# Seven tile products for eight in part of an fp32 down projection, with a new head and tail

## The reference

```
h = h + relu(RMSNorm(h) @ W_up)^2 @ W_down      # W_up 2048 x 8192, W_down 8192 x 2048
out = RMSNorm(h)
```

## Time and profile before

| | |
|---|---|
| three executions | 2035.08, 2036.14, 2038.41 us; median 2036.14 |
| the profiled execution | 2037.86 us |
| its span | 2036.1 us |
| granted TensorE clock, mean | 0.998 |
| instructions | 26601 |
| weight loads of the down projection | 128 of 512 KB, median 4.8 us from issue to landing |
| of the up projection | 128 of 512 KB, 3.9 us |

### The profile page before, as it was taken

The page is one execution under the profiler, slowest core; times in us unless marked ns, Lnnn a source line. Parts: engine busy times, 40 slices in busy tenths (PEclk is TensorE's granted clock), DMA queues, the critical chain, the costliest instruction groups (busy, mean ns, idle before and its releaser), DMA issues.

```text
span 2036.1 us, 26601 instructions
## 1 busy us (share of the span) xinstructions
PE 2018.9 (99%) x9378; PEld 1666.9 (82%) x9378; DVE 1384.1 (68%) x1735; ACT 1034.7 (51%) x1454; POOL 278.6 (14%) x417
## 2 busy tenths in 40 slices
PE   9999999999999999999999999999999999999997
PEld 7888888888888877888887888888888888888886
DVE  6665878687665678885688877666556556655664
ACT  5444546464544567663566644544344434433443
POOL 4000111111110233330033311011001000000000
PEclk9999999999999999999999999999999999999999
DMA  8757666666666666666666677766666666666663
GB/s 274 219 178 208 195 194 191 195 192 192 175 208 208 183 191 198 193 197 209 183 185 185 194 255 233 229 211 204 215 195 203 223 197 193 221 205 185 219 216 135
DMA packets 202726, 411.49 MB, mean 202 GB/s; under 512 B 15264, under 2 KB 15360, under 8 KB 201200
## 3 DMA queue, kind: packets, MB, share of 16 engines
q1 hardware_dynamic: 188656, 364.56, 58.0%
q0 software_dynamic: 13776, 44.96, 7.6%
q10 hardware_dynamic: 176, 0.40, 0.1%
HBM read 379.91 MB, written 2.16 MB: 188 GB/s over the span
## 4 chain that ended last, share of the span: by engine, by line
PE 91%; DVE 3%; ACT 2%; issue 2%; ACTq 1%; DVEq 0%; POOLq 0%; POOL 0%; DMA 0%
PE acc L307 28%; PE acc L309 28%; PE acc L308 28%; DVE lo L274 1%; PE x L999 1%; ACT hi L268 1%; ACT W L1313 1%; PE tr L948 1%; PE tr L342 1%; PE x L931 1%; DVE XCT L1697 0%; PE x L937 0%; PE x L867 0%; ACTq L1314 0%; PE tr L950 0%
## 5 line engine op out<-in xcount | busy, mean ns | idle before, releaser
L274 DVE TENSOR_TENSOR lo<-raw,hi 128x1024 fp32r<-128x1024 f32 x688 | 837.8, 1233 | 457.9 <-ACT hi L268 450.0
L268 ACT ACTIVATE hi<-raw 128x1024 fp32r<-128x1024 f32 x688 | 718.8, 1057 | 623.3 <-PE acc L309 561.4
L307 PE MATMUL acc<-hi,LAh 128*128 128x512 f32 x1840 | 727.9, 396 | 0.0
L309 PE MATMUL acc<-hi,LAl 128*128 128x512 f32 x1840 | 717.3, 390 | 0.0
L308 PE MATMUL acc<-lo,LAh 128*128 128x512 f32 x1840 | 716.6, 389 | 0.0
L307 PEld LDWEIGHTS acc<-hi,LAh 128*128 128x128 f32 x1840 | 345.5, 188 | 75.3 <-issue 3.2
L309 PEld LDWEIGHTS acc<-hi,LAl 128*128 128x128 f32 x1840 | 345.3, 188 | 73.1
L308 PEld LDWEIGHTS acc<-lo,LAh 128*128 128x128 f32 x1840 | 345.6, 188 | 70.6 <-issue 1.1
L307 PE MATMUL acc<-hi,LBh 128*128 128x512 f32 x896 | 349.8, 390 | 0.0
L309 PE MATMUL acc<-hi,LBl 128*128 128x512 f32 x896 | 348.7, 389 | 0.0
L308 PE MATMUL acc<-lo,LBh 128*128 128x512 f32 x896 | 348.6, 389 | 0.0
(11 more groups left out here) (343 smaller groups left out, 1324.4 us busy)
## 6 DMA issues: line engine op xcount, KB each, us to landing
raw<-w_in SPq DMA_DIRECT2D x304, 512.0 KB, 4.3
raw<-w_up SPq DMA_DIRECT2D x128, 512.0 KB, 3.9
raw<-w_down SPq DMA_DIRECT2D x128, 512.0 KB, 4.8
raw<-w_proj_ssm SPq DMA_DIRECT2D x64, 512.0 KB, 4.7
raw<-w_proj_nsa SPq DMA_DIRECT2D x32, 512.0 KB, 4.7
raw<-w_out SPq DMA_DIRECT2D x32, 512.0 KB, 5.5
W<-acs_rows POOLq DMA_DIRECT2D x8, 1024.0 KB, 6.7
W<-TB POOLq DMA_DIRECT2D x48, 128.0 KB, 4.1
```

The lines of the kernel that those rows point to most:

```text
L268: act.activation(hi[:, sl, :, :], raw[:, sl, :, :], ACT.Copy).then_inc(s_hi, 1)
L274: dve.tensor_tensor(lo[:, sl, :, :], raw[:, sl, :, :], hi[:, sl, :, :].bitcast(F32), ALU.subtract).then_inc(s_lo, 1)
L307: pe.matmul(o, xh, wh, start=(k == 0), stop=False)
L309: x = pe.matmul(o, xl, wh, start=False, stop=(k == KT - 1))
```

## The change

A chunk pair and a depth pair of blocks (tiles j = 0 and 1, that is blocks 0 to 3) together with the two row halves form a 2 x 2 by 2 x 2 product of tiles. The change makes it with seven products for eight (Winograd's form of Strassen's scheme), for two of the eight depth pairs of seven of the eight chunk pairs: both pairs of phases 0 to 2 and the first of phase 3.

- A pair of chunks ("quad") is now 20 ring positions: four ordinary tiles of the first chunk (n, j = 2 to 5), a group a, b, p, q, two ordinary tiles (j = 6, 7), a second group, and six ordinary tiles of the second chunk. a and b are the loaded tiles of the same depth in both chunks; VectorE makes p and q from them in their ring slots with four half-tile additions. p and q aren't loaded. Of b only the second half is split.
- The seven products go to acc and to the four banks B1, B6, B7, B5. Sums of the activation's row tiles are made and split once a phase (slots 13 to 15). In slots 13 to 17 of a quad VectorE adds the product banks into H (first_sums to fourth_sums).
- The load of a tile into the slot of an a waits for one low part more, that of b.
- ScalarE's and VectorE's loops over phases 1 and 2 are written out. XDT and ZT are no longer kept in the MLP; the row sums' parts lie there.
- Head: POOL makes the identity first, TensorE warms from then on (9, 8 and 12 transposes), the first tile is split in two halves, x(1) and x(2) are turned after the first and second tile, and SP's order of loads is changed to match.
- Tail: POOL's power is replaced by a square root on ScalarE (with one such root ahead of the last phase) and a reciprocal and one Newton step on VectorE (root_inverse); the second half's output is scaled and stored in four pieces.

```diff
+UP, QUAD, TWO = 32, 20, 16
+PHASE = UP + 2 * QUAD
+G_MLP = 8 * C_MLP
+G_END = G_MLP + 3 * PHASE + UP + QUAD + TWO
+QUAD_ORDER = ([("n", 0, j) for j in (2, 3, 4, 5)] + [(c, 0, 0) for c in "abpq"] + [("n", 0, j) for j in (6, 7)] +
+              [(c, 0, 1) for c in "abpq"] + [("n", 1, j) for j in (2, 3, 4, 5, 6, 7)])
+TWO_ORDER = [("n", c, j) for c in range(2) for j in range(8)]
+def tile_of(i, x):
+    if x < UP:
+        return "n", x // 8, x % 8, x // 4 + 1
+    q, y = divmod(x - UP, QUAD)
+    order = TWO_ORDER if (q == 1 and i is LAST) else QUAD_ORDER
+    kind, c, j = order[y]
+    loads = UP // 4 + 4 * q + sum(order[z][0] not in "pq" for z in range(y % 4, y + 1, 4))
+    return kind, 4 + 2 * q + (c if kind == "n" else 0), j, loads
+LAST = 3
...
+        SF = TH
+        U3, U5, U2, U4 = (GA[:, 1, NC * n:NC * (n + 1)] for n in range(4))
+        U35 = GA[:, 1, 0:2 * NC].rearrange("p (n c) -> p n c", n=2)
+        B1, B6, B7, B5 = TR[0], TR[1], X6, X7
...
             load_group(sp, C_KC, 0, w_in, 0, KC0)
+            load_group(sp, C_KC, 1, w_in, 0, KC0)
             load_x(1)
-            load_group(sp, C_KC, 1, w_in, 0, KC0)
             load_group(sp, C_KC, 2, w_in, 0, KC0)
             load_x(2)
             load_group(sp, C_KC, 3, w_in, 0, KC0)
-            load_group(sp, C_KC, 4, w_in, 0, KC0)
             load_x(3)
-            for j in (5, 6, 7):
+            for j in (4, 5, 6, 7):
...
+            def load_tile(sp, i, x):
+                kind, c, j, _ = tile_of(i, x)
+                if kind in "pq":
+                    return
+                before = tile_of(i, x - RING)[0] if x >= RING else "n"
+                sp.wait_ge(s_lo, G_MLP + PHASE * i + x - RING + (2 if before == "a" else 1))
+                if c < 4:
+                    src = w_up[:, 2 * j:2 * j + 2, ds(D * i + NC * c, NC)]
+                else:
+                    c0 = NC * (c - 4 + (kind == "b"))
+                    src = w_dn[:, ds(KT * i + 2 * j, 2), c0:c0 + NC]
+                sp.dma_start(raw[:, x % RING, :, :], src).then_inc(s_raw[x % RING], 16)
+            def load_phase(sp, i):
+                for x in range(PHASE if i is not LAST else PHASE - 4):
+                    load_tile(sp, i, x)
+            with sp.Fori(0, 3) as i:
+                load_phase(sp, i)
+            load_phase(sp, LAST)
...
+            pool.affine_select(identf[:, :], identf[:, :], [[-1, P]], ALU.not_equal, 1.0, base=0, channel_multiplier=1)
+            pool.drain().then_inc(s_idn, 1)
...
-            for t in range(2):
-                pool.wait_ge(s_v, t + 2)
-                pool.tensor_tensor(RS[:, t:t + 1], VV[:, t:t + 1], mhalf[:, 0:1], ALU.pow).then_inc(s_fr, 1)
...
+            pe.wait_ge(s_idn, 1)
+            warm(9)
...
-            warm(9)
+            warm(8)
             turn_x(0)
-            warm(5)
-            turn_x(1)
-            mm_chunk(pe, C_KC, 0, LAh, LAl, {0: [lambda: turn_x(2)], 3: [lambda: turn_x(3)]},
-                     need={0: [(s_x0, 1)], 1: [(s_trd, 1)], 2: [(s_trd, 2)], 4: [(s_trd, 3)], 6: [(s_trd, 4)]})
+            warm(12)
+            pe.wait_ge(s_x0, 1)
+            pe.wait_ge(s_g0l, 1)
+            mm_chunk(pe, C_KC, 0, LAh, LAl, {0: [lambda: turn_x(1)], 1: [lambda: turn_x(2)], 3: [lambda: turn_x(3)]},
+                     need={1: [(s_trd, 1)], 2: [(s_trd, 2)], 4: [(s_trd, 3)], 6: [(s_trd, 4)]})
...
+            def product(o, xh, xl, g, kk, start, stop):
+                sl = g % RING
+                pe.matmul(o[:, :], xh, hi[:, sl, kk, :], start=start, stop=False)
+                pe.matmul(o[:, :], xh, lo[:, sl, kk, :], start=False, stop=False)
+                return pe.matmul(o[:, :], xl, hi[:, sl, kk, :], start=False, stop=stop)
+            def seven_products(g, u, p0, p1):
+                def rows(t, k):
+                    return LAh[:, 2 * u + k, t * P:(t + 1) * P], LAl[:, 2 * u + k, t * P:(t + 1) * P]
+                def sums(n):
+                    return LSh[:, n - 1, u * P:(u + 1) * P], LSl[:, n - 1, u * P:(u + 1) * P]
+                one, two = u == 0, u == 1
+                pe.wait_ge(s_lo, g + 1)
+                product(B1, *rows(0, 0), g, 0, one, two)
+                product(acc[p0][0], *rows(0, 1), g, 1, False, two).then_inc(s_mm, 1)
+                pe.wait_ge(s_lo, g + 2)
+                product(acc[p1][0], *sums(4), g + 1, 1, one, False).then_inc(s_mm, 1)
+                pe.wait_ge(s_lo, g + 3)
+                product(B5, *sums(1), g + 2, 0, one, two)
+                product(B7, *sums(3), g + 2, 1, one, two).then_inc(s_mm, 1)
+                pe.wait_ge(s_lo, g + 4)
+                product(B6, *sums(2), g + 3, 0, one, two)
+                product(acc[p0][1], *rows(1, 1), g + 3, 1, False, two).then_inc(s_mm, 1)
+            def four_blocks(i, q):
+                g, C = G_MLP + PHASE * i + UP + QUAD * q, C_MLP + 8 * i + 4 + 2 * q
+                p0, p1 = C % 2, (C + 1) % 2
+                pe.wait_ge(s_acc, C - 1)
+                for y, (kind, c, j) in enumerate(QUAD_ORDER):
+                    if kind == "a":
+                        if j == 0:
+                            pe.wait_ge(s_acc, C)
+                            pe.wait_ge(s_sfl, i + 1)
+                            if 2 * i + q:
+                                pe.wait_ge(s_ux, 2 * i + q)
+                        seven_products(g + y, j, p0, p1)
+                    elif kind == "n":
+                        if c == 0 and j == 6:
+                            pe.wait_ge(s_trd, E_MLP + 4 * i + 4)
+                        mlp_group(g + y, (p0, p1)[c], j, LAh, LAl, t_first=((j == 2 and c == 0), j == 2), last=((c, j) == (1, 7)))
...
+            act.wait_ge(s_raw[0], 16)
+            act.activation(hi[:, 0, 0, :], raw[:, 0, 0, :], ACT.Copy).then_inc(s_g0h, 1)
...
+                kind, _, u, loads = tile_of(i, x)
+                g, sl = G_MLP + PHASE * i + x, x % RING
+                if kind in "pq":
+                    act.wait_ge(s_wt, 8 * i + 4 * ((x - UP) // QUAD) + 2 * u + (1 if kind == "p" else 2))
+                else:
+                    act.wait_ge(s_raw[sl], 16 * (2 * C_MLP + 16 * i + loads))
+                act.wait_ge(s_mm, g - RING + 1)
+                k0 = 1 if kind == "b" else 0
+                act.activation(hi[:, sl, k0:2, :], raw[:, sl, k0:2, :], ACT.Copy).then_inc(s_hi, 1)
...
+            def split_tile(i, x):
+                kind, _, u, loads = tile_of(i, x)
+                g, sl = G_MLP + PHASE * i + x, x % RING
+                sa, sb_, sp_, sq = ((x - "abpq".find(kind) + n) % RING for n in range(4))
+                if kind == "a":
+                    dve.wait_ge(s_lo, g - 1)
+                    for n in (sa, sb_):
+                        dve.wait_ge(s_raw[n], 16 * (2 * C_MLP + 16 * i + tile_of(i, x + (n == sb_))[3]))
+                    for kk, (m, mk) in enumerate(((sa, 0), (sb_, 0))):
+                        y = dve.tensor_tensor(raw[:, sp_, kk, :], raw[:, sb_, kk, :], raw[:, m, mk, :], ALU.subtract)
+                    y.then_inc(s_wt, 1)
+                if kind == "b":
+                    dve.wait_ge(s_lo, g - 1)
+                    dve.wait_ge(s_wt, 8 * i + 4 * ((x - UP) // QUAD) + 2 * u + 1)
+                    dve.tensor_tensor(raw[:, sq, 0, :], raw[:, sp_, 1, :], raw[:, sa, 0, :], ALU.add)
+                    dve.drain()
+                    dve.tensor_tensor(raw[:, sq, 1, :], raw[:, sa, 1, :], raw[:, sq, 0, :], ALU.subtract).then_inc(s_wt, 1)
+                dve.wait_ge(s_hi, g + 1)
+                k0 = 1 if kind == "b" else 0
+                dve.tensor_tensor(lo[:, sl, k0:2, :], raw[:, sl, k0:2, :], hi[:, sl, k0:2, :].bitcast(F32),
+                                  ALU.subtract).then_inc(s_lo, 1)
+            def row_sums(i):
+                r = [TSS[0].rearrange("p (a q r j) -> p r q a j", q=2, r=4, j=32)[:, n, :, :, :] for n in range(4)]
...
+                dve.drain()
...
+            def row_sums_low(i):
+                dve.wait_ge(s_sfh, i + 1)
+                dve.tensor_tensor(LSl[:, :, :], SF, LSh[:, :, :].bitcast(F32), ALU.subtract).then_inc(s_sfl, 1)
+            def add_blocks(g, C, n):
+                dve.wait_ge(s_mm, g)
+                dve.drain()
+                for t in range(2):
+                    x = dve.tensor_tensor(H[:, t, NC * n:NC * (n + 1)], acc[C % 2][t][:, :], H[:, t, NC * n:NC * (n + 1)], ALU.add)
+                x.then_inc(s_acc, 1)
+            def first_sums(n):
...
+                dve.tensor_tensor(h, B1[:, :], h, ALU.add)
+                dve.tensor_copy(U2, B1[:, :])
+                dve.drain()
+                dve.tensor_tensor(U2, B6[:, :], U2, ALU.add)
+            def second_sums():
+                dve.drain()
+                dve.tensor_tensor(U3, B7[:, :], U2, ALU.add)
+                dve.tensor_tensor(U4, B5[:, :], U2, ALU.add)
+            def third_sums(n):
+                h = H[:, 0, NC * n + NC:NC * n + 2 * NC]
+                dve.drain()
```

(66 more changed lines are left out.)

159 lines of the change are left out of this document (105 added, 54 removed).

## The result

The changed kernel took **2062.43 us** (median of four executions, 2059.20 to 2065.27) against 2036.39 of the kernel before (four, 2035.08 to 2038.41): the ratio is 1.0127, with a 95% interval of 1.0115 to 1.0140. The forecast was 2065.0 and slower.

What follows compares the result with a forecast made beforehand. TensorE was taken to set the pace. Stalls of 38.4 us less 9.5 gained give +28.9, head and tail 0: 2066.8 from the profiled 2037.9, or 2065.0 at the median's level; range 2050 to 2087.

Steps and rivals of the forecast that it cites:

- The bound and the 42 matmuls: MLP: TensorE alone sets the pace; 42 matmuls removed at 0.227 us each gain 9.5 us if its feeders stay ahead.
- the marks that were named: Signs of being right: 42 fewer matmuls, MLP idle 38 us, pauses 2.5 to 3.5, w_down wait over 30, first-quad q 2.
- the pause before q in first quads: First quads: q waits behind the split of the last activation block on ScalarE and VectorE, 2.1 us.
- The long pause: Every quad: TensorE waits for the first ordinary tile behind the second group's q, 2.8 us.
- The chain: Reload behind the second group: issue, landing, high part, low part, TensorE's start, against at most 3.5 us of matmuls in store.
- The sum of a first quad: First quad of a phase: all its TensorE stalls together, 6.4 us.
- The small ones: Second group: b 0.65 (second quads 0.25), p 0.45 us; second quads' tile behind the first group 0.7 us.
- The sum: MLP: stalls of four first quads at 6.4 and three second quads at 4.2 us, 38.4 us lost.
- the quick end: MLP: every landing at 3.7 us with quicker drains, +20 us; as the case of cheap stalls 2056, chance 0.15.
- The clock: MLP: granted clock falls after seven long pauses, up to 3 us each; half, 11, gives 2076, all 2087; chance 0.12.
- Head: Start of the kernel: first matmul from 10.74 to about 9.7 us, offset by later transposes; net 0, -1.5 to +1.1.
- Tail: End of the kernel: factor 0.5 us later without POOL's 0.55 us power, regained by smaller output pieces; net 0, within 0.7.

Runs made afterwards that it cites:

- Experiment 1: Changed kernel with q made from b instead of a, so a's slot reloads without waiting for b's low part (wrong output): 2044.62 us, 1.0035.
- experiment 2: Changed kernel without folding the four product banks into H (output lacks those products): 2056.01 us, 1.0091.
- experiment 3: Changed kernel with 16 transposes of 128 columns on TensorE in the pause behind each second group's q: 2054.62 us, 1.0082.
- Experiment 5: Changed kernel with the load order of the head as before the change: 2060.82 us, 1.0116.
- experiment 8: Changed kernel, order a, b, n, p, q, p's sums behind a's low part, new head but x's last part loaded behind the fifth weight tile: 2029.71 us, 0.9970.
- experiments 4: Changed kernel with an ordinary tile between b and p, q in a's slot, loads waiting only for their own slot: 2033.21 us, 0.9984.
- 6: Changed kernel with the tail as before the change, POOL's power included: 2060.31 us, 1.0121.
- 7: Changed kernel with order a, b, n, p, q, p's sums behind a's low part, and the head as before the change: 2028.09 us, 0.9961.

## Why the prediction was right, and where not

**The bound and the 42 matmuls.** As forecast: TensorE set the pace, the matmuls removed were worth 9.5, and the lead was lost. Of the marks that were named, three came: 42 fewer matmuls, the w_down wait from 5 us to over 30, and the longest pauses ahead of the first tile behind every second q, though of 2.25 to 2.56 us for 2.5 to 3.5. A second long pause came in the four first quads and in one second quad. TensorE's idle time in the MLP was 24 us for 38, and the pause before q in first quads did not come.

**The long pause.** Forecast 2.8, measured 2.25 to 2.56. The chain had the right links and length (6.9 us for 6.8; the landing was 4.3 where 4.1 was taken); b's low part ended 4.4 us before TensorE ran dry, 4.0 in the sum. Experiment 1 shows that its cause is the wait of the load for b, experiment 2 that it is not VectorE's work.

**The pause ahead of q in first quads** (2.1) was the step that failed. It didn't come. ScalarE in the kernel after:

```profile
1417.59 0.69 ACT L1519 ACTIVATE XR<-acc,RS 128x512 f32<-128x512 f32 x1 [1.66 <-PE acc L1150]
...
1427.30 1.06 ACT L440 ACTIVATE LAh<-XTOK 128x1024 fp32r<-128x1024 f32 x1 [0.48 <-DMA XTOK<-W]
1428.47 1.06 ACT L1531 ACTIVATE hi<-raw 128x1024 fp32r<-128x1024 f32 x1
```

The forecast took over the 12.56 us from the first-rows activation to the last activation block, as if they were fixed. Here they are 9.7: the wait for the spreads is 0.48 us, where it was 3.34. Tile XTOK of the kernel after, 1422 to 1426:

```profile
L425 POOL DMA_DIRECT2D XTOK<-W x4: 543/564/583, 1422.8 to 1424.4; - x4
...
DMA to landing us min/median/max: 2.5/2.7/2.8
```

Those of the earlier trace rows took 2.5, 4.3 and 5.6 (least, median, most). Between 1414.6 and 1428.1 no weight load was issued here, because p and q are not loaded; so the spreads had the queues to themselves. The same holds in all four phases (at most 2.9 us, and up to 5.8 before). The block came early enough for q: its low part ended at 1431.36, and TensorE began q at 1431.68.

The tile behind that q was 1.6 to 1.8 us late, where 0.35 was forecast on top of the 2.1. The block has no part in it. VectorE in the kernel after:

```profile
1420.46 2.08 DVE L416 STREAM_TRANSPOSE W<-Y 128x512 f32<-128x512 f32 x2
...
1423.57 1.28 DVE L2095 TENSOR_TENSOR raw<-raw 128x512 f32<-128x512 f32 x2
...
1427.27 1.82 DVE L2105 TENSOR_TENSOR lo<-raw,hi 128x512 fp32r<-128x512 f32 x2
```

From 1418.32 to 1422.54 VectorE is at the rows and blocks of the last up chunk. So p's sums start 6.2 us after the quad's first matmul (1417.33), for 4.7 in the sum, and b's low part ends at 10.6 for 9.5. The load waits for it, goes at 1428.14 and lands at 1432.35; the block's splits (1427.30 to 1430.23) are over by then. The forecast worked out a second quad and took a first one's start for the same. The sum of a first quad (6.4) came out near 4.1.

**The small ones.** The second group's b and p (0.65 + 0.45, and 0.25 + 0.45 in second quads) were forecast as pauses and were none over 0.3 us, but for one of 0.34. The tile behind the first group of second quads (0.7) was in time in two of three; in the third a landing of 6.2 us cost 2.3. In the second quad of the first phase (from 1465.76) both come from landings: b's tile had landed 3.1 us after the start for 4.6 in the sum, so its low part ended at 7.6 for 9.5, and the second b took 3.9 us from issue to landing for 4.7.

**The sum** of the pauses, with the small gaps, is 26.2 + 2.9 = 29.1 for 38.4 (the terms as given, 4 x 6.4 + 3 x 4.2, make 38.2), near the quick end that had been given (+20 net, or 29.5 gross).

**The clock.** The forecast held this a rival with 0.12, at half of 3 us for each of seven pauses, 11 us; it happened after five of the eight pauses of over 2 us, for 1.6 us each, 8.1 in all, and experiment 3 confirms the amount. So the total of 37.2 for 38.4 is nearly right by luck, by two errors that cancel: stalls 9 us too dear, the clock left out at 8. The forecast's own mark for it, a granted clock below 0.99, was too coarse: the mean of the MLP reads 0.99 and that of the span 0.995.

**Head.** Forecast net 0 (-1.5 to +1.1). The first matmul did come early, at 9.43 (forecast 9.7, before 10.74), but the fifth tile began 2.1 us later than before, at 25.52. In the rows of SP's issues x's last part now goes at 4.73 and lands at 19.80, and the fifth weight tile goes at 9.91 and lands at 23.03; before, the tile landed at 17.57 and x at 19.12. What the step missed is this swap on SP's queue. ScalarE at the head, after:

```profile
23.05 2.03 ACT L300 ACTIVATE hi<-raw 128x1024 fp32r<-128x1024 f32 x2 [4.72 <-DMA raw<-w_in]
```

Experiment 5 (the old head) has 23.44 again, and 1.6 us less in all, with intervals that overlap. With the new head the fifth tile began anywhere from 22.60 to 25.60 in six traces, with the old one at 23.42 to 23.44 in three. I compared the starts of equal matmuls with those of the kernel before: from 62 us to about 715 us the lag against it doesn't move by 0.1 us, and but for experiment 8 it is the lag of the fifth tile. There it is +2.1 in the kernel after, +2.2, +1.7, +0.4 and +1.7 in experiments 1 to 4, -0.8 in 6, all with the new head, and 0.0 in 5 and 7 with the old one (+0.6 in 8, with the other order of loads). So the new head cost 1.2 us in the mean of its six traces, where the forecast had 0, and the first matmul, 1.3 us earlier, bought nothing.

The first MLP matmul (1325.3 to 1332.2) no longer shows it, for steps of 1.1 to 1.4 us lie between, at six places from 766 to 1162 us, which come in one execution and not in another, with the old head and the new. At each TensorE has two matmuls that may wait for VectorE's Y. Before, it did so here:

```profile
765.46 1.10 PE L988 MATMUL x<-Y,XCT 128*128 128x512 f32 x2 [0.66 <-DVE Y L1806]
```

The matmul behind this pair came 2.1 us after the one ahead of it, in the kernel after 0.7. Of the 4.7 us between experiments 8 and 7, 0.6 stand at 715 us, and most of the rest are such steps.

**Tail.** Forecast net 0, within 0.7; measured -1.95. Timeline of VectorE there, after:

```profile
2056.27 0.15 DVE L2213 TENSOR_SCALAR VV<-SS 128x1 f32<-128x1 f32 x1
...
2057.46 0.16 DVE L2225 TENSOR_TENSOR RS<-SS 128x1 f32<-128x1 f32 x1
2057.74 1.02 DVE L2236 TENSOR_SCALAR GB<-GB,RS 128x640 f32<-128x640 f32 x2
```

From the end of the variance to the scaling 1.32 us pass, where it was 0.67: the factor is 0.65 later, for 0.5 in the forecast. The pieces gave nothing back: from the start of the scaling to the last landing it takes 5.4 us, where it took 4.9. What was mis-sized is POOL's power, priced at its own 0.55 us. At the end of the program each engine drains, and the line of POOL's drain (kernel before, then kernel after; duration in ns, start in us) reads:

```profile
L98 POOLq DRAIN  x1: 8767/8767/8767, 2027.1 to 2027.1; - x1
```
```profile
L120 POOLq DRAIN  x1: 9003/9003/9003, 1969.5 to 1969.5; - x1
```

Before, POOL's drain begins with its last power, at 2027.13, and ends at 2035.90. The last landing (2032.67) and all other drains (the latest ends at 2032.9) are over by then; only the closing semaphore events of the engines follow it, until 2036.12. Now POOL's last work is the spreads: its drain ends at 1978.46, and the span ends at 2063.51, 0.4 us behind the last landing instead of 3.45. In experiment 6, with the power back, it is 8.77 us of drain and 3.46 again. So the -1.95 are +0.65 for the factor, +0.45 up to the last landing, and -3.05 for POOL. No run takes the power and the pieces apart; the order of the events in these traces does.

## What to carry to other kernels

Fewer matmuls pay only while the feeders keep their lead. For each slot that is filled by computing instead of loading, work out the next load's chain (release, landing, both splits) against the matmuls in store; if it is longer, put ordinary work between the pieces before giving up the scheme, as experiments 4 and 7 did with the same arithmetic. A wait moved into an in-order list holds what stands behind it, so an operation that needs a late tile goes behind the work that doesn't. And a small job on an engine that is otherwise done can set the end of the kernel: look at what that engine still has to do behind it.
